# A two-layer decoder trunk on one core: channel statistics in columns, a new order of the last attention pairs, and depthwise-convolution taps moved between input products

## What is computed

```python
h = x * (1 + sc1) + sh1                    # modulated input, from silu(c) @ w_ada
z = h @ w_in                               # q, k, v (8 heads x 64), g (2 x 512 channels)
q, k = rope(q) * HEAD_DIM ** -0.5, rope(k)
o = dilated window attention               # (128,1), (512,4), (2048,16), softmax-merged
u = ga * sigmoid(gb)
cz = silu(layernorm(causal_dwconv_31(u)))  # over 512 channels
mix = concat(rms(o) * beta_attn, rms(cz) * beta_conv) @ w_out
x = layernorm(alpha * x + g1 * mix)
h = x * (1 + sc2) + sh2
x = layernorm(alpha * x + g2 * ((silu(h @ w_gate) * (h @ w_up)) @ w_down))
```

## Time and profile before

| | |
|---|---|
| runs | 1645.03, 1647.55, 1648.67 us (median 1647.55) |
| profiled execution | 1650.15 us |
| its span, first to last instruction | 1648.4 us |
| TensorE busy | 1526.2 us (93%) |
| VectorE busy | 790.7 us (48%) |
| ScalarE busy | 561.6 us (34%) |
| GpSimd busy | 81.9 us (5%) |
| DMA | 197.16 MB, mean 120 GB/s |
| mean granted clock of TensorE | 0.954 of full speed |

### The profile page before, as it was taken

One profiled execution on the slowest core, in us unless ns is written; L12 is line 12 of the kernel. 1 busy time (PEld: TensorE's weight loads), 2 busy tenths in 40 slices (PEclk: granted clock), 3 DMA queues, 4 the chain that ended last, 5 costly groups with the idle time before them and its releaser, 6 DMA issues.

```text
span 1648.4 us, 26440 instructions
## 1 busy us (share of the span) xinstructions
PE 1526.2 (93%) x11456; PEld 1380.1 (84%) x11456; DVE 790.7 (48%) x1246; ACT 561.6 (34%) x884; POOL 81.9 (5%) x104
## 2 busy tenths in 40 slices
...
DMA packets 59523, 197.16 MB, mean 120 GB/s; under 512 B 22544, under 2 KB 22928, under 8 KB 48400
## 3 DMA queue, kind: packets, MB, share of 16 engines
...
## 4 chain that ended last, share of the span: by engine, by line
PE 82%; DVE 11%; ACT 3%; issue 1%; DMA 1%; SPq 0%; DVEq 0%; ACTq 0%
PE ps L1230 66%; PE ps L1250 3%; PE ps L1321 3%; DVE sb_y L869 2%; DVE sb_x L980 1%; PE ps L1358 1%; PE ps L1332 1%; DMA sb_big<-w_ada 1%; ACT sb_E L588 1%; PE ps L1379 1%; PE ps L1587 1%; PE ps L1259 1%; DVE sb_x L953 1%; DVE sb_w_lo L831 1%; PE ps L1310 1%
## 5 line engine op out<-in xcount | busy, mean ns | idle before, releaser
L1230 PE MATMUL ps<-sb_h,sb_w_hi 128*128 128x288 f32 x4224 | 766.0, 297 | 3.0 <-DVE sb_x L920 3.0
L1230 PEld LDWEIGHTS ps<-sb_h,sb_w_hi 128*128 128x128 f32 x4224 | 623.1, 188 | 52.0 <-issue 47.4
L1230 PE MATMUL ps<-sb_h,sb_w_lo 128*128 128x288 f32 x2112 | 450.6, 294 | 0.0
L831 DVE TENSOR_TENSOR sb_w_lo<-sb_w_raw,sb_w_hi 128x1024 fp32r<-128x1024 f32 x192 | 235.7, 1229 | 375.5 <-ACT sb_w_hi L507 375.1
L1230 PEld LDWEIGHTS ps<-sb_h,sb_w_lo 128*128 128x128 f32 x2112 | 339.6, 188 | 0.0
L507 ACT ACTIVATE sb_w_hi<-sb_w_raw 128x1024 fp32r<-128x1024 f32 x192 | 202.1, 1053 | 324.1 <-PE ps L1230 290.5
L869 DVE SCALAR_TENSOR_TENSOR sb_y<-sb_uP,sb_vec,sb_y 128x512 f32<-128x512 f32 x240 | 164.8, 743 | 0.5
L1230 PE MATMUL ps<-sb_a_hi,sb_w_hi 128*128 128x288 f32 x704 | 151.9, 296 | 0.0
L1230 PE MATMUL ps<-sb_a_hi,sb_w_lo 128*128 128x288 f32 x704 | 150.1, 294 | 0.0
L1230 PE MATMUL ps<-sb_a_lo,sb_w_hi 128*128 128x288 f32 x704 | 149.6, 293 | 0.0
L795 ACT ACTIVATE sb_a_hi<-sb_af 128x576 fp32r<-128x576 f32 x44 | 30.2, 686 | 267.1 <-DVE sb_af L1185 267.1
...
## 6 DMA issues: line engine op xcount, KB each, us to landing
...
sb_ring<-w_ada SPq DMA_DIRECT2D x40, 1024.0 KB, 5.8
...
sb_ring<-vc_d SPq DMA_DIRECT2D x12, 1024.0 KB, 6.9
sb_big<-w_ada SPq DMA_DIRECT2D x8, 1024.0 KB, 12.2
sb_ring<-kc_d SPq DMA_DIRECT2D x8, 1024.0 KB, 7.4
...
sb_cache_a<-kc_d SPq DMA_DIRECT2D x4, 1024.0 KB, 8.0
```

The costliest lines, as they stand in the source:

```text
L831: nc.vector.tensor_tensor(w_lo[:, g % NW, :], w_raw[:, g % NR, :], w_hi[:, g % NW, :].bitcast(F32), ALU.subtract)\
L1230: ins = nc.tensor.matmul(z[:, i], a[:, g % NW, w], b[:, k0 + k, i * H:(i + 1) * H], start=first and k == 0 and t == 0, stop=last and k == ...
```

## The change

1. Maxima: `tensor_tensor_reduce` gives the scaled, negated maximum itself (scale -SCALE, min in place of max). The small `tensor_scalar` behind it is gone (L1018, L1035), the exponentials take scale -1, and each waits for its own block, not for a pair of blocks.
2. Taps: TAPS is a table per layer now, with more taps between input products; TAPS_TAIL goes from 8, 8, 8 to 2, 6, 6.
3. Order of the tail on TensorE, ScalarE and VectorE (below). The column sums of the convolution go to other banks.
4. The statistics of the convolution and of both rms norms go in columns: `token_rows` (sums of squares, four channel tiles to four groups of 32 partitions), a copy, `token_cols`, root and reciprocal on 96x6 or 96x12, `spread`. The squares of the Silu outputs move from ScalarE to VectorE; the rms factor of the convolution reaches SBUF by a ScalarE copy.
5. At the end of a layer ScalarE does `norm_last` before the weight's split.
6. Modulated input: `take_rest` of tiles 5 and 6 moves in front of the first `normalise`, the low part of the weight from behind tile 1 to behind tile 4, the scaling on ScalarE goes a tile ahead.

```diff
@@ ACT, exps
-                    act.wait_ge(s["nm_ready"], nth(l, "nm_ready", p * QB + q))
+                    act.wait_ge(s["s_free"], nth(l, "s_free", p * 2 * QB + i))
@@ ACT, tail
                 act.wait_ge(s["c_sum"], l + 1)
-                nc.scalar.activation(halves(meanc[:]), CONV_STAT, ACT.Copy, scale=1.0 / DA).then_inc(s["c_mean"], 1)
-                sample_outputs(l, 2)
+                nc.scalar.activation(halves(meanc[:]), C_SUM, ACT.Copy, scale=1.0 / DA).then_inc(s["c_mean"], 1)
+                outputs(l, 3)
                 for c in range(CT):
                     act.wait_ge(s["c_cent"], nth(l, "c_cent", c))
                     nc.scalar.activation(sqc[:, c], y[:, c], ACT.Square).then_inc(s["c_sq"], 1)
+                    if c == 1:
+                        sample_turned(l, 2)
+                act.wait_ge(s["c_rows"], l + 1)
+                nc.scalar.activation(halves(rowsc[:]), C_STAT, ACT.Copy).then_inc(s["c_rows_sb"], 1)
+                sample_exps(l, 3)
+                nc.scalar.preload_act_table(ACT.Sqrt)
+                sample_outputs(l, 2)
+                act.wait_ge(s["c_var"], l + 1)
+                nc.scalar.activation(c_sd_col, C_COLS, ACT.Sqrt, scale=1.0 / (GW * DA), bias=eps[0:TW]).then_inc(s["c_sd"], 1)
+                nc.scalar.preload_act_table(ACT.Silu)
                 sample_own(l, 2)
                 sample_turned(l, 3)
...
@@ ACT, end of a layer
+                norm_last(l, 1)
                 split(l, UL + 2)
-                norm_last(l, 1)
@@ DVE, maxima
                         nc.vector.tensor_tensor_reduce(E[:, e, E_OFF[q]:E_OFF[q] + w], ps[:, 4 + i % 3, 0:w], mp[:, SEQ - w:SEQ],
-                                                       1.0, LEAST, ALU.add, ALU.max, mx8[p % 2][:, i:i + 1]).then_inc(s["s_free"], 1)
...
-                    nc.vector.tensor_scalar(nm8[p % 2][:, two], mx8[p % 2][:, two], -SCALE, None, ALU.mult).then_inc(s["nm_ready"], 1)
+                                                       -SCALE, MOST, ALU.add, ALU.min, nm8[p % 2][:, i:i + 1]).then_inc(s["s_free"], 1)
@@ DVE, tail
                 dve.wait_ge(s["c_sd"], l + 1)
-                st.link(nc.vector.reciprocal(rstdc[:], sdc[:]))
+                nc.vector.reciprocal(c_rstd_col, c_sd_col).then_inc(s["c_rcol"], 1)
...
+                dve.wait_ge(s["c_spread"], l + 1)
                 for c in range(CT):
-                    nc.vector.tensor_tensor(y[:, c], y[:, c], rstdc[:], ALU.mult).then_inc(s["c_norm"], 1)
-                dve.wait_ge(s["p_sd"], l + 1)
-                st.link(nc.vector.reciprocal(rstdm[:, 0:SEQ], sdm[:, 0:SEQ]))
+                    nc.vector.tensor_tensor(halves(y[:, c, :]), halves(y[:, c, :]), C_STAT, ALU.mult).then_inc(s["c_norm"], 1)
@@ PE
+            def token_rows(dst, src, i):
+                for c in range(CT):
+                    g = slice(c * GW, (c + 1) * GW)
+                    ins = nc.tensor.matmul(dst[g, i], ones[:, 0:GW], src[:, c, i * H:(i + 1) * H], start=True, stop=True)
+                return ins
+            def token_cols(dst, rows_sb):
+                for j in range(TG):
+                    ins = nc.tensor.matmul(dst[:, j:j + 1], rows_sb[:, j * TW:(j + 1) * TW], ones[:, 0:1], start=True, stop=True)
+                return ins
+            def spread(dst, col):
+                for j in range(TG):
+                    half, o = divmod(j * TW, H)
+                    ins = nc.tensor.matmul(dst[:, half, o:o + TW], col[:, j:j + 1].to_broadcast([TW, P]), eye[0:TW, 0:TW],
+                                           start=True, stop=True)
+                return ins
@@ tables
-TAPS = [0, 0, 0, 5, 5, 5, 5, 5, 3, 2, 0, 0, 5, 7, 0, 5, 9, 0, 5, 7]
+TAPS = [[0, 0, 0, 5, 5, 5, 5, 5, 3, 5, 4, 0, 6, 7, 0, 8, 12, 0, 7, 7],
+        [0, 0, 0, 5, 5, 5, 5, 5, 3, 2, 0, 0, 6, 7, 0, 8, 12, 0, 7, 7]]
-TAPS_TAIL = [8, 8, 8]
+TAPS_TAIL = [2, 6, 6]
```

More of the change, by code:

```diff
@@ L282, in trunk @@
         var_col, sd_col, rstd_col = (cols[0:TW, j] for j in range(3))
+        c_sd_col, c_rstd_col, ratio_col = (ccols[0:TW, j] for j in range(3))
+        m_sd_col, m_rstd_col = (ccols[0:TW, j:j + 2].rearrange("p c j -> p (c j)") for j in (3, 5))
         def halves(t):
@@ L526, in high @@
                     nc.scalar.activation(h_hi[:, k, :], hf[:, k % HF, :], ACT.Copy).then_inc(s["h_hi"], 1)
[L528 to L531 removed]
+                for kt in range(2):
+                    scaled(kt)
+                    high(kt)
+                scaled(2)
+                for kt in range(3, KT):
                     scaled(kt)
@@ L855, in modulate @@
                             .then_inc(s["h_lo"], 1)
-                    if kt == 1 and ahead:
+                    if scale and kt + 2 < KT:
+                        scale(kt + 2)
+                    if kt == 4 and ahead:
                         ahead[-1]()
@@ L966, in norm_last @@
                 nc.vector.reciprocal(rstd_col, sd_col).then_inc(s["ln_rcol"], 1)
-                for k in range(3, 5):
+                for k in range(3, KT - 1):
                     take_rest(l, q, k)
```

189 lines of the change are left out of this document (90 added, 99 removed).

## The result

The changed kernel took 1597.37 us (median of four runs, 1596.76 to 1598.96) against 1647.26 (four runs, 1645.03 to 1648.67): a ratio of 0.970, with a 95% interval of 0.9683 to 0.9717. The profiled execution took 1596.85 us, its span is 1595.1 (1648.4 before), the mean granted clock 0.970 (0.954 before). TensorE is busy 1508.3 us, VectorE 767.0, ScalarE 557.5. Two executions lie far outside the rest, one of e9 (2123.75 us) and one of the kernel before beside e9 to e11 (3748.04), and count in no comparison here.

A forecast was written before the change was run, and what follows sets the result against it. TensorE was taken as the bound (82% of the chain), with gains only where it waits. Terms -17.1, -15.1, -1.2, -9.35, -6.0 and -1.5 sum to -50.25: 1650.15 becomes 1599.9, 1597 us as a median; range 1588 to 1610.

The forecast's parts named there:

- Up to the column sums: Front of the tail: column sums start 15.6 us earlier, column mean 14.8; layer 1's last six taps come 2.1 later.
- From the mean to the first output products: Tail, statistics in columns: ScalarE becomes the limit and the first output products start 16.0 us earlier in layer 0.
- Second half: Tail, second half of the first output products: 1.1 us gained ahead of it, 2.0 behind it without the last reciprocal.
- D: Tail, between the two halves of the first output products: 7.8 us counted against 8.87 before; sign: 7 to 8.
- E: Tail, second half's start to the third output product: 7.8 us instead of 9.77, TensorE's own products the limit.
- Clock discount: Tail: 2 us taken off each layer's gain because column sums move next to a stretch at 0.50 clock.
- Rival 1: The new tail runs at half clock, costing some 8 us a layer in place of 2: 1609 us; chance 0.15.
- Boundary: End of layer 0: norm before weight split, row sums to first normalised tile 7.60 us instead of 16.95: -9.35.
- Modulated inputs: Start of the modulated inputs: three places gain 2.15 us each, layer 0's first modulate loses 0.5: -6.0 in all.
- End: End of the kernel: two take_rest less between the last tiles, -1.5 us.
- Input products: Input products: direct negative maxima gain 0.6 us a layer, added taps cost nothing if they fit: -1.2 in all.
- Rivals 2 and 4: First, a transfer becomes the tail's new wait: 1607 us, chance 0.10; second, products get a lower clock: 1697 us, 0.04.

The follow-up runs named there:

- e9: The changed kernel with 31 matmuls a layer added that only keep TensorE busy in four waits of the tail: 1595.62 us.
- e11: The changed kernel with two more table loads a layer in ScalarE's queue ahead of the first output products: 1603.09 us.
- e3: The changed kernel with the convolution's column sums put back behind pair 3's work, other engines' order to fit: 1609.51 us.
- e5: The changed kernel with the tables of taps as they were before, one for both layers: 1608.80 us.
- e10: The changed kernel with ScalarE's squares of the prompt's attention output split, three of four channel tiles done earlier: 1595.40 us.
- e4: The changed kernel with the convolution's variance over whole rows again, both rms norms still in columns: 1601.67 us.
- e8: The changed kernel with a spare reciprocal over 576 columns on VectorE at the end of the tail: 1602.57 us.
- e1: The changed kernel with ScalarE's split of the next weight back in front of the norm at a layer's end: 1606.92 us.
- e2: The changed kernel with the modulated input's order as it was before the change: 1606.87 us.
- e7: The changed kernel with small multiplications by 1 back behind the row and sample maxima, exponentials waiting for them: 1602.25 us.
- e6: The changed kernel with layer 0's table of taps used for layer 1 too: 1600.20 us.

## Why the prediction was right, step by step

- **The total.** 1597 was forecast, 1597.37 came. Between the medians the gain is 49.9, and 50.25 was forecast. But the terms were read from the profiled execution, and between the profiled executions 53.3 us were gained, 3.0 more than the sum has. The forecast carried over that the profiled execution of before lies 2.6 above its median (1650.15); that of after lies 0.5 below its own. The two errors cancel, and that the number fits to 0.4 us is luck: more was gained than the terms say in the modulated inputs (2.4, the start among them), at the boundary (0.5) and in the input products (0.5), less in the tails (0.4).
- **Up to the column sums: right.** Column sums 21.1 us behind the keys' issue (forecast 21), mean done 26.5 behind the last input product (26.55), narrow sums done 32.5 behind (32.5). The keys landed when taken (10.2), and layer 1's 2.1 for its last taps was 2.15. e3 shows that the order is worth 4 to 7 us a layer, e5 that it needs the taps moved.
- **From the mean to the first output products: a little mis-sized.** 1.2 us of gain were forecast from the column mean on, and 0.8 came: 21.8 us before, 21.0 after. B is counted from the end of the column sums, 0.7 us ahead of the mean before and 1.4 after, and is 22.5 and 22.4. The first output products start 47.5 us behind the last input product (forecast 47.1). The limit was named rightly as ScalarE's queue (e10, e11), but the prompt's squares and pair 2's and 3's copies, which were done elsewhere before, stand in it now. The narrow sums took 1.18 where 1.1 was taken. Undone alone, the convolution's statistics cost 2.2 (e4), more than the whole step gained. That they pay for the crowding that the new order makes on ScalarE is argued, not shown.
- **Second half: mis-sized.** Forecast gains 1.1 and 2.0, measured 0.3 and 1.1. D is 8.5 where 7.8 was counted, outside the 7 to 8 that the prediction named as a sign. E is 8.7 where 7.8 was taken: TensorE's products, at low clock, are the limit, and at that clock the late reciprocal is worth 0.6 (e8). Where E is 7.9 to 8.2, nearly what was taken, the clock was higher, so what fails in this term is the clock.
- **Clock discount: right size, wrong place.** 2 us a layer were taken off for column sums at half clock. In the profile they ran at full clock. The two halves lost it: C took 8.9 where 8.06 had been carried over and e9 has 6.6, and E 8.7 where 7.8 was taken, together 1.8 a layer. Rival 1, at 0.15, did not come at its price of 12 us, and the tail's clock rose from 0.87 to 0.91. What it names is a part of every execution, though: A varies by 3.6 us with it. The rule on transposes (the Trainium skill, TensorE: Matmul & The Clock Gate, the part on transpose mode) would, as the prediction used it, have kept the front at half clock; 228 to 232 ran at 1.00. Transposes are only about 1 of the 2.8 us that TensorE is busy there, so this weighs against that use and does not test the rule itself.
- **Boundary: right**, 9.35 and 2.15 forecast for both, 12.0 measured; the tiny matmuls at full clock (1.10 for 2.05) are more than the excess. e1 returns 8.7 and e2 2.2. **Modulated inputs:** 2.8 and 3.2 for 2.15; how much of the excess is the clock's, no run separates (e2). The fifth product step starts 10.6 us after the first normalise (10.3 forecast, 12.44 before). The 0.5 forecast against the first place can't be told from the start's scatter. **End:** 1.4 for 1.5.
- **Input products:** 1.2 forecast, 1.7 measured; e7 gives 2.0 to the small multiplications, so that term was too small. The taps fitted in layer 0; that more do not fit in layer 1 (e6) is something that the prediction did not say.
- **Rivals 2 and 4.** The keys are on the chain, a new wait of 2.6, but at their forecast time; the sample values never held TensorE. The products' clock stayed at 1.00.
